# Making the low part of a weight tile one tile later than its high part, in a ten-stage fp32 network

## The chip, the cores and the metric

The kernel runs on one NeuronCore of a Trainium2 chip. The metric is the device time of one execution in microseconds (us). The engines are TensorE (PE, matrix products; PEld is its weight load), VectorE (DVE), ScalarE (ACT), GpSimd (POOL) and SyncE (SP, which here only issues DMAs). Each engine works through its own instruction stream strictly in order, so an instruction that waits for another engine also holds up everything behind it on its own.

## The reference, cut to what matters

256 tokens of width 1024 go through ten stages in float32: feed-forward, dilated attention, feed-forward, feed-forward, retention, feed-forward, and then twice a mixer and an MLP.

```python
def swiglu(h, w_gate, w_up, w_down):
    return (jax.nn.silu(h @ w_gate) * (h @ w_up)) @ w_down

# first block: two layers; the mixer is dilated attention, then retention
    h = swiglu(rms_norm(x, g[0]), ffn_w_gate[i, 0], ffn_w_up[i, 0], ffn_w_down[i, 0])   # 1024 -> 2816 -> 1024
    x = x + 0.5 * rms_norm(h, g[1])
    hm = rms_norm(x, g[2])
    m = dilated_attention(hm, ...) if i == 0 else retention(hm, ...)                    # hm @ w_in, heads, @ w_out
    x = x + rms_norm(m, g[3])
    h = swiglu(rms_norm(x, g[4]), ffn_w_gate[i, 1], ffn_w_up[i, 1], ffn_w_down[i, 1])
    x = x + 0.5 * rms_norm(h, g[5])

# second block: two layers
    dq, dk, dv, c_q, c_kv_kr, xq, gate_logits = jnp.split(h @ w_in[l], split_idx, axis=-1)
    y_diff = diff_attention(dq, dk, dv, ...) @ w_diff_o[l]       # q, k normed per head and rotated
    y_mla = latent_attention(c_q, c_kv_kr, ...) @ w_mla_o[l]
    y_mem = memory_cross_attention(xq, mem_n, w_mem_kv[l], ...) @ w_cross_o[l]
    merged = gates[:, :, 0] * y_diff + gates[:, :, 1] * y_mla + gates[:, :, 2] * y_mem
    x = x + merged @ w_out[l]
    x = x + jnp.square(jax.nn.relu(rmsnorm(x, g_mlp[l]) @ w_mlp1[l])) @ w_mlp2[l]
```

Every `@` with a weight matrix streams that matrix from memory once.

## The kernel before, in words

**Weights.** All weights are cut into 744 tiles, most of them 128 x 1024 float32 (512 KB), numbered in the order in which PE multiplies with them. A float32 product is made from three products of shorter numbers, so each tile is split in two. For tile i:

- SP loads it into `w_raw` (four buffers, `RAW`), once the low part of tile i-4 is made, which was the last to read that buffer;
- ACT copies it, rounded, into `w_hi` (L2205; four buffers, `SPLIT`), once PE has finished tile i-4;
- DVE makes `w_lo = w_raw - w_hi` (L2517), once `w_hi` is made. In the attention part of a mixer POOL does it for every second tile (L3240);
- PE does three matmuls for each 128-wide chunk: high x high, low x high, high x low (L1926, L1927, L1928; other places with the same pattern are L1952/L1953/L1961, L1909/L1910/L1915 and L1990/L1991/L1992). The first of the three waits for `w_lo` of the tile.

A 128 x 1024 tile keeps PE busy for some 2.8 us.

**The order.** The order of all work is planned once, as one list of steps (`self.plan`). Each engine's program goes through the whole list and issues the part of a step that is its own. So the list sets the order within each engine, and semaphores hold engines together. When PE's step of tile i has been planned, `tile_used(i)` plans `split(i + 4)`, one step that holds ACT's high part, DVE's or POOL's low part and SP's next load (tile i+8). At the end of a stage these steps can be held back (`hold_last`, `held`, `release`), so that they come after the work of the seam. Tiles which are multiplied in two halves of the tokens (`first_half`) are not followed by a split of their own.

**What lies between.** Attention steps are put into the same list between weight tiles by generators that take turns: on DVE these are evacuations of PSUM (L2559, L2575), norms (L3009, L3030, L3049), rotations of queries and keys (L3088 to L3096, six operations a half), maxima and scores (L2712), and in the dilated stage the weights of the three groups (L2822 to L2839). The exponentials stand on ACT (L2322, L2331, L2369), small powers on POOL (L3221).

**Tiles by stage.** 0 to 65 feed-forward, 66 to 145 dilated attention (on PE 217 to 511 us), 146 to 277 two feed-forwards, 278 to 357 retention (896 to 1161 us), 358 to 423 feed-forward, 424 to 519 first mixer (1350 to 1687 us), 520 to 583 MLP, 584 to 679 second mixer (1869 to 2206 us), 680 to 743 MLP. In the first mixer 436 is the second tile of the joint latent projection, 439 to 446 are queries, 447 to 454 keys, 455 to 462 values.

Of the kernel before, what the change touches and what calls it, by code (L numbers as in the profile page):

```python
# [399 lines left out]
class Kernel:  # L400


    def __init__(self, nc, a, stages):
# [49 lines left out]

        self.tiles, self.blocks, self.uid = [], 0, 0
        self.hold_at, self.held = None, []
        self.share, self.act_share, self.flip = 0, 2, 0
        self.gain_plan, self.gain_at = self.gains_in_order(), 0
        self.x_event = [[("x", 0, h, c) for c in range(2)] for h in range(HALVES)]
# [81 lines left out]
        return self.gain_at - 1  # L540

    def split(self, i):
        self.step("split", i, "pool" if self.share and i % self.share == 0 else "dve")

    def tile_used(self, i):
        if i == self.hold_at or self.held:
            self.held.append(i + SPLIT)
        else:
            self.split(i + SPLIT)
# [27 lines left out]
        return b  # L577

    def first_half(self, t, kind):
        self.tiles.append(t)  # L580
        self.tail.append((kind, len(self.tiles) - 1))
        self.step(kind, len(self.tiles) - 1, 0)
        yield
# [119 lines left out]
    def order(self):  # L703
        self.step("setup")
        self.step("load_x", 0)
        self.step("load", 0)
        self.step("load_x", 1)
        for i in range(1, RAW):
            self.step("load", i)
        self.step("next_gain", 1, [("x", 0, HALVES - 1, 1), ("w_raw", 1)])  # L710
        self.step("masks")
        for n, (kind, i, j) in enumerate(self.stages):
            self.st = n
            self.act_share = 3 if kind == "mix" else 2
            self.share = 0
            self.following = self.stages[n + 1] if n + 1 < len(self.stages) else None
            dict(ffn=self.ffn, mlp=self.mlp, dilated=self.dilated, retention=self.retention, mix=self.mix)[kind](i, j)
        for c in range(2):
            for half in range(HALVES):
                self.pending(half, c)  # L720
                self.step("store", half, c, self.x_event[half][c])
        self.plan = [s for s in self.plan if s[0] not in ("split", "load") or s[1] < len(self.tiles)]
        self.plan = [s for s in self.plan if s[0] != "next_gain" or s[1] < len(self.gain_plan)]


# [392 lines left out]
    def dilated(self, i, j):  # L1118
        a = self.a
        self.feed(order="classes")  # L1120
        self.step("masks_seen")
        q, k = self.put("da_q", 0, [P, HALVES, D]), self.put("da_k", 8, [P, HALVES, D])
        pairs = [(self.put(f"da_qt{n}", at, [P, DC, SEQ]), self.put(f"da_kt{n}", at + 8, [P, DC, SEQ])) for n, at in enumerate((16, 72))]
# [223 lines left out]
    def retention(self, i, j):  # L1347
# [17 lines left out]

        def qkv():
            bs = yield from self.pair_of_blocks(self.xt, (w_in, 0), (w_in, BLOCK))
            got["q"] = [[] for _ in range(HALVES)]
            for c, b in enumerate(bs):
                for half in range(HALVES):  # L1370
                    self.step("evac", Evac(b, half, self.by_turns(), q[:, half, c * BLOCK:(c + 1) * BLOCK], []))
                    got["q"][half].append(("evac", b.uid, half))
            got["k"] = yield from self.project(self.xt, w_in, D, D, k, D)
            got["v"] = yield from self.project(self.xt, w_in, D, H_R * DV_R, v, 2 * D)
# [176 lines left out]
    def mix(self, layer, _):  # L1551
# [20 lines left out]
        low = self.tok  # L1572
# [15 lines left out]
            mem_over.append(self.last_tile())  # L1588

        self.feed(memory_kv)  # L1590

        def projections():
            part = lambda name, dst, after=(): self.project(self.xt, w_in, D, IN_SIZES[name], dst, IN_AT[name], after)
# [242 lines left out]
def sp_program(k):  # L1836
    sp, q, ev = k.nc.sync, Queue(k.nc.sync), k.ev
    for what, *of in k.plan:
        if what == "load_x":
            c, = of  # L1840
            for half in range(HALVES):
                src = k.a["x"][0, half * P:(half + 1) * P, c * BLOCK:(c + 1) * BLOCK]
                sp.dma_start(k.x[:, half, c * BLOCK:(c + 1) * BLOCK], src).then_inc(*ev.mark(k.x_landed[half][c], ("x", 0, half, c), by=16))

        if what == "load":
            i, = of
            t = k.tiles[i]
            dst = k.raw[i % RAW][:, 0:t.nk * t.n].rearrange("p (k n) -> p k n", k=t.nk)
            if i >= RAW:
                q.wait_ge(*(yield from ev.of("w_lo", i - RAW)))  # L1850
            sp.dma_start(dst, t.view).then_inc(*ev.mark(k.w_landed[i % RAW], ("w_raw", i), by=16))
        if what == "split":
            i = of[0] + RAW
            if i < len(k.tiles):
                t = k.tiles[i]
                dst = k.raw[i % RAW][:, 0:t.nk * t.n].rearrange("p (k n) -> p k n", k=t.nk)
                q.wait_ge(*(yield from ev.of("w_lo", i - RAW)))
                sp.dma_start(dst, t.view).then_inc(*ev.mark(k.w_landed[i % RAW], ("w_raw", i), by=16))
        if what == "store":
            half, c, x_event = of  # L1860
            cols = slice(c * BLOCK, (c + 1) * BLOCK)
            q.wait_ge(*(yield from ev.of(*x_event)))
            q.wait_ge(*(yield from ev.of("masks")))
            sp.dma_start(k.out[0, half * P:(half + 1) * P, cols], k.x[:, half, cols]).then_inc(*ev.mark(k.out_stored, ("out", half, c), by=16))
        yield STEP
    q.wait_ge(*(yield from ev.of("out", HALVES - 1, 1)))
# [316 lines left out]
def act_program(k):  # L2183
# [8 lines left out]
    for what, *of in k.plan:  # L2192
# [3 lines left out]
                cols = slice(c * BLOCK, (c + 1) * BLOCK)  # L2196
                act.dma_start(k.gain_tile[0][:, cols], k.gain_plan[0][cols].partition_broadcast(P)).then_inc(*ev.mark(sem, (name, 0), by=16))

        if what == "split":
            i = of[0]  # L2200
            m = k.tiles[i].nk * k.tiles[i].n
            q.wait_ge(*(yield from ev.of("w_raw", i)))
            if i >= SPLIT:
                q.wait_ge(*(yield from ev.of("tile", i - SPLIT)))
            act.activation(k.w_hi[i % SPLIT][:, 0:m], k.raw[i % RAW][:, 0:m], ACT.Copy).then_inc(*ev.mark(k.w_hi_made, ("w_hi", i)))  # L2205
# [167 lines left out]
        if what == "oct_keep" and of[2] == "act":  # L2373
            o, s, _, dst = of
# [120 lines left out]
def dve_program(k):  # L2495
    dve, q, ev = k.nc.vector, Queue(k.nc.vector), k.ev
# [10 lines left out]
    for what, *of in k.plan:  # L2507
# [1 line left out]
            dve.memset(k.probs.free[0][0][:, :], 0.0).then_inc(*ev.mark(k.dve_done, ("fill_ready",)))  # L2509
            dve.memset(k.minus_half[:, :], -0.5).then_inc(*ev.mark(k.dve_done, ("minus_half",)))  # L2510

        if what == "split" and of[1] == "dve":
            i = of[0]
            m = k.tiles[i].nk * k.tiles[i].n
            q.wait_ge(*(yield from ev.of("w_hi", i)))
            hi, lo, raw = k.w_hi[i % SPLIT][:, 0:m], k.w_lo[i % SPLIT][:, 0:m], k.raw[i % RAW][:, 0:m]
            dve.tensor_tensor(lo, raw, hi.bitcast(F32), ALU.subtract).then_inc(*ev.mark(k.w_lo_made, ("w_lo", i)))  # L2517
# [278 lines left out]
        if what == "oct_keep" and of[2] == "dve":  # L2796
            o, s, _, dst = of
# [8 lines left out]
        if what in ("two_weights", "weights"):  # L2806
# [9 lines left out]
            low = k.da_low[:, at, :] if two else nm[:, 1, at, :]  # L2816
# [40 lines left out]
        if what == "combine":  # L2857
            o, s = of
# [356 lines left out]
def pool_program(k):  # L3215
# [7 lines left out]
    for what, *of in k.plan:  # L3223
# [8 lines left out]
            pool.dma_start(k.causal[:, :], a["c_causal"]).then_inc(*ev.mark(k.masks_landed, ("masks",), by=16))  # L3232
            q.wait_ge(*(yield from ev.of("minus_half")))

        if what == "split" and of[1] == "pool":
            i = of[0]
            m = k.tiles[i].nk * k.tiles[i].n
            q.wait_ge(*(yield from ev.of("w_hi", i)))
            hi, lo, raw = k.w_hi[i % SPLIT][:, 0:m], k.w_lo[i % SPLIT][:, 0:m], k.raw[i % RAW][:, 0:m]
            pool.tensor_tensor(lo, raw, hi.bitcast(F32), ALU.subtract).then_inc(*ev.mark(k.w_lo_pool, ("w_lo", i)))  # L3240
# [155 lines left out]
```

## Time and profile before

| | |
|---|---|
| time, median of 3 runs | 2388.45 us (2387.96 to 2388.94) |
| profiled execution: span | 2387.5 us |
| PE busy | 2351.7 us, 98% |
| PE's weight loads busy | 2020.1 us, 85% |
| DVE busy | 1511.0 us, 63% |
| ACT busy | 1195.5 us, 50% |
| POOL busy | 283.9 us, 12% |
| PE's granted clock | full (digit 9) in all 40 slices |
| memory read | 171 GB/s over the span |

The span runs from the first to the last recorded instruction of one execution; the timed runs lie 0.5 to 1.4 us above it. PE is busy nearly all the time, so a wait shows as a small gap on PE, and the sum of these gaps is what another order could win. DVE and ACT have idle time that costs nothing unless PE waits for what stands behind it.

### The profile page before, as it was taken

To read this page: it belongs to the slowest core of one execution; us is meant where nothing else is said; L and a number is where in the kernel's file an instruction comes from. 1 tells how busy PE (TensorE), PEld (TensorE's weight loads), DVE (VectorE), ACT (ScalarE), POOL (GpSimd) and SP (SyncE) were. 2 spreads that over 40 slices of the span, in tenths; PEclk is the share of its full clock that TensorE was granted. 3 is DMA by queue.
4 is the path that set the end of the run, shared out by engine and by line. 5 is a ranking of instruction groups with operands and counts; after the bars stand their busy time and mean duration, and the time that the engine had idled before them with its cause. 6 is when DMAs were issued, how large, how long until landed. Compare 5 with 4: busy or idle time off the path is not lost.

```text
span 2387.5 us, 34279 instructions
## 1 busy us (share of the span) xinstructions
PE 2351.7 (98%) x13900; PEld 2020.1 (85%) x13900; DVE 1511.0 (63%) x2307; ACT 1195.5 (50%) x1794; POOL 283.9 (12%) x247
## 2 busy tenths in 40 slices
PE   9999999999999999999999999999999999999999
PEld 8987778779979977777899887788998887888987
DVE  6555567776555658666665677756665687656654
ACT  4444454454444446444544565555554555554543
POOL 1100010000000000000001121434110122333000
PEclk9999999999999999999999999999999999999999
DMA  7755644466566656544666654445666554445554
GB/s 229 209 194 175 172 125 136 148 187 183 186 194 177 186 185 197 173 134 151 184 186 204 203 177 143 124 126 183 186 199 206 181 170 131 121 144 172 183 189 145
DMA packets 263278, 411.66 MB, mean 172 GB/s; under 512 B 13770, under 2 KB 129370, under 8 KB 263120
## 3 DMA queue, kind: packets, MB, share of 16 engines
q1 hardware_dynamic: 256256, 389.59, 53.2%
q0 software_dynamic: 6432, 19.28, 3.1%
q8 instruction: 110, 1.80, 0.3%
q10 hardware_dynamic: 432, 0.59, 0.1%
q14 instruction: 48, 0.39, 0.1%
HBM read 408.31 MB, written 1.10 MB: 171 GB/s over the span
## 4 chain that ended last, share of the span: by engine, by line
PE 85%; DVE 8%; ACT 4%; issue 1%; POOL 1%; DMA 0%; SPq 0%; ACTq 0%; DVEq 0%
PE banks L1926 16%; PE banks L1928 16%; PE banks L1927 16%; PE banks L1952 9%; PE banks L1961 9%; PE banks L1953 9%; DVE w_lo L2517 2%; ACT w_hi L2205 2%; PE banks L2015 1%; PE banks L2075 1%; PE banks L2028 1%; DVE probs L2712 1%; PE banks L1909 1%; PE banks L1910 1%; PE banks L1915 1%
## 5 line engine op out<-in xcount | busy, mean ns | idle before, releaser
L2517 DVE TENSOR_TENSOR w_lo<-w_raw,w_hi 128x1024 fp32r<-128x1024 f32 x688 | 838.9, 1225 | 618.1 <-ACT w_hi L2205 616.9
L2205 ACT ACTIVATE w_hi<-w_raw 128x1024 fp32r<-128x1024 f32 (+2 forms) x744 | 777.8, 1049 | 534.6 <-PE banks L1928 379.5
L1926 PE MATMUL banks<-w_hi,xt_hi 128*128 128x512 f32 (+2 forms) x1056 | 432.3, 409 | 7.0 <-DVE xt_lo L2545 3.6
L1952 PE MATMUL banks<-xt_hi,w_hi 128*128 128x256 f32 x1728 | 426.5, 283 | 4.7 <-DVE w_lo L2517 3.1
L1953 PE MATMUL banks<-xt_hi,w_lo 128*128 128x256 f32 x1728 | 425.2, 283 | 0.0
L1928 PE MATMUL banks<-w_hi,xt_lo 128*128 128x512 f32 (+2 forms) x1056 | 413.3, 391 | 0.0
L1927 PE MATMUL banks<-w_lo,xt_hi 128*128 128x512 f32 (+2 forms) x1056 | 412.4, 391 | 0.0
L1952 PEld LDWEIGHTS banks<-xt_hi,w_hi 128*128 128x128 f32 x1728 | 326.6, 189 | 6.6 <-DVE w_lo L2517 3.4
L1953 PEld LDWEIGHTS banks<-xt_hi,w_lo 128*128 128x128 f32 x1728 | 326.7, 189 | 0.0
L1926 PEld LDWEIGHTS banks<-w_hi,xt_hi 128*128 128x128 f32 x1056 | 198.9, 188 | 52.3 <-DVE w_lo L2517 9.0
L1961 PE MATMUL banks<-xt_lo,w_hi 128*128 128x256 f32 x1728 | 243.0, 282 | 0.0
L1928 PEld LDWEIGHTS banks<-w_hi,xt_lo 128*128 128x128 f32 x1056 | 198.9, 188 | 45.4
L1927 PEld LDWEIGHTS banks<-w_lo,xt_hi 128*128 128x128 f32 x1056 | 199.5, 189 | 41.8 <-issue 3.1
L1961 PEld LDWEIGHTS banks<-xt_lo,w_hi 128*128 128x128 f32 x1728 | 222.7, 189 | 0.0
L3221 POOL TENSOR_TENSOR stat<-stat,minus_half 128x1 f32<-128x1 f32 (+2 forms) x60 | 56.4, 944 | 1036.9 <-DVE stat L2505 549.2
L3240 POOL TENSOR_TENSOR w_lo<-w_raw,w_hi 128x1024 fp32r<-128x1024 f32 x56 | 134.5, 2402 | 263.8 <-ACT w_hi L2205 263.8
L1926 PE MATMUL banks<-w_hi,ffn_ht_hi 128*128 128x512 f32 x320 | 127.3, 398 | 0.0
L1928 PE MATMUL banks<-w_hi,ffn_ht_lo 128*128 128x512 f32 x320 | 126.5, 395 | 0.0
L1927 PE MATMUL banks<-w_lo,ffn_ht_hi 128*128 128x512 f32 x320 | 125.7, 393 | 0.0
L1928 PE MATMUL banks<-w_hi,mlp_ht_lo 128*128 128x512 f32 x256 | 101.7, 397 | 0.0
L1927 PE MATMUL banks<-w_lo,mlp_ht_hi 128*128 128x512 f32 x256 | 101.1, 395 | 0.0
L1926 PE MATMUL banks<-w_hi,mlp_ht_hi 128*128 128x512 f32 x256 | 100.9, 394 | 0.0
(438 smaller groups left out, 3042.4 us busy)
## 6 DMA issues: line engine op xcount, KB each, us to landing
w_raw<-in_w_mlp SPq DMA_DIRECT2D x128, 512.0 KB, 3.7
w_raw<-in_w_in SPq DMA_DIRECT2D x104, 512.0 KB, 3.7
w_raw<-in_ffn_w_gate SPq DMA_DIRECT2D x88, 512.0 KB, 3.9
w_raw<-in_ffn_w_up SPq DMA_DIRECT2D x88, 512.0 KB, 4.2
w_raw<-in_ffn_w_down SPq DMA_DIRECT2D x88, 512.0 KB, 3.6
w_raw<-in_attn_w_in SPq DMA_DIRECT2D x72, 512.0 KB, 3.8
w_raw<-in_ret_w_in SPq DMA_DIRECT2D x64, 512.0 KB, 3.8
w_raw<-in_ret_w_out SPq DMA_DIRECT2D x16, 512.0 KB, 3.8
```

What stands on the lines that cost most here:

```text
L1909: pe.matmul(bank, xh, hi[:, j * t.n:(j + 1) * t.n], start=(c == 0), stop=False)
L1910: pe.matmul(bank, xh, lo[:, j * t.n:(j + 1) * t.n], start=False, stop=False)
L1926: pe.matmul(bank, xh, wh, start=(c == 0), stop=False)
L1927: pe.matmul(bank, xh, wl, start=False, stop=False)
L1928: mm = pe.matmul(bank, xl, wh, start=False, stop=(c == b.chunks - 1))
L1952: pe.matmul(out[f], hi[:, cols], xh, start=(c == 0), stop=False)
L1953: pe.matmul(out[f], lo[:, cols], xh, start=False, stop=False)
L1961: mm = pe.matmul(out[f], hi[:, cols], xl, start=False, stop=(c == DC - 1))
L2205: act.activation(k.w_hi[i % SPLIT][:, 0:m], k.raw[i % RAW][:, 0:m], ACT.Copy).then_inc(*ev.mark(k.w_hi_made, ("w_hi", i)))
L2517: dve.tensor_tensor(lo, raw, hi.bitcast(F32), ALU.subtract).then_inc(*ev.mark(k.w_lo_made, ("w_lo", i)))
L3221: pool.tensor_tensor(out, mean, k.minus_half[:, 0:n], ALU.pow).then_inc(*ev.mark(k.pool_done, name))
L3240: pool.tensor_tensor(lo, raw, hi.bitcast(F32), ALU.subtract).then_inc(*ev.mark(k.w_lo_pool, ("w_lo", i)))
```

## The change

`split` is divided: the step "high" holds ACT's part, the step "low" DVE's or POOL's part and SP's load. With `low_later` set, the low part of a tile is put in the list only after the high part of the next tile; without it, straight behind its own, as before. It is set in the dilated stage from the end of `feed` on (the first tile concerned is 69), in retention from the end of the first pair of blocks on (tile 290), in the mixers from the end of the memory projection on (tiles 436 and 596). It is taken back at the start of every stage. Low parts that are due are put in the list at once where splits are held back and ahead of a tile in two halves.

```diff
@@ planner @@
     def split(self, i):
-        self.step("split", i, "pool" if self.share and i % self.share == 0 else "dve")
+        self.step("high", i)
+        self.low_parts()
+        self.low_due.append((i, "pool" if self.share and i % self.share == 0 else "dve"))
+        if not self.low_later:
+            self.low_parts()
+
+    def low_parts(self):
+        for i, by in self.low_due:
+            self.step("low", i, by)
+        self.low_due = []
 
     def tile_used(self, i):
         if i == self.hold_at or self.held:
+            self.low_parts()
             self.held.append(i + SPLIT)
         else:
             self.split(i + SPLIT)
@@ first_half @@
     def first_half(self, t, kind):
+        self.low_parts()
         self.tiles.append(t)
@@ order, for each stage @@
+            self.low_later = False
@@ dilated @@
         self.feed(order="classes")
+        self.low_later = True
@@ retention, qkv @@
             bs = yield from self.pair_of_blocks(self.xt, (w_in, 0), (w_in, BLOCK))
+            self.low_later = True
@@ mix @@
         self.feed(memory_kv)
+        self.low_later = True
@@ SP program @@
-        if what == "split":
+        if what == "low":
             i = of[0] + RAW
@@ ACT program @@
-        if what == "split":
+        if what == "high":
@@ DVE program; POOL program alike @@
-        if what == "split" and of[1] == "dve":
+        if what == "low" and of[1] == "dve":
```

The order of PE's, ACT's and SP's own instructions stays what it was. DVE's changes (180 low parts stand elsewhere), and POOL's in three places a mixer. In the rows below `w_lo0` to `w_lo3` are the four buffers: tile i is in buffer i mod 4.

DVE in the first mixer, at the joint latent projection: `w_lo0` is tile 436, `w_lo1` 437, `mx_ck` the normed keys of the memory; L2517 and L3049 become L2533 and L3065. Before:

```order
L2505 TENSOR_SCALAR stat17_97<-norm_sums1_105 128x4
L2517 TENSOR_TENSOR w_lo0_57<-w_raw0_49,w_hi0_53 128x864
L3049 TENSOR_TENSOR mx_ck0_216<-banks,stat16_96 128x512
L3049 TENSOR_TENSOR mx_ck0_216<-banks,stat18_98 128x512
L2517 TENSOR_TENSOR w_lo1_58<-w_raw1_50,w_hi1_54 128x864
L2517 TENSOR_TENSOR w_lo2_59<-w_raw2_51,w_hi2_55 128x576
```

and now:

```order
L2521 TENSOR_SCALAR stat17_97<-norm_sums1_105 128x4
L3065 TENSOR_TENSOR mx_ck0_216<-banks,stat16_96 128x512
L3065 TENSOR_TENSOR mx_ck0_216<-banks,stat18_98 128x512
L2533 TENSOR_TENSOR w_lo0_57<-w_raw0_49,w_hi0_53 128x864
L2533 TENSOR_TENSOR w_lo1_58<-w_raw1_50,w_hi1_54 128x864
L2575 TENSOR_SCALAR tok_64<-banks,row_scale_65 128x384
L2533 TENSOR_TENSOR w_lo2_59<-w_raw2_51,w_hi2_55 128x576
```

The low part of tile 436 stood ahead of the two `mx_ck` operations and now stands behind them; that of 438 has moved behind the evacuation of `tok`.

DVE in the same mixer, between the first and the second half of the key rotation (`mx_k`), where `w_lo3` is tile 459, `w_lo0` 460, `w_lo1` 461 and `w_lo2` 462. Before:

```order
L2517 TENSOR_TENSOR w_lo0_57<-w_raw0_49,w_hi0_53 128x1024
L3088 TENSOR_TENSOR tmp0_70<-mx_k0_207,rope_k_120 128x512
L3089 TENSOR_TENSOR tmp1_71<-mx_k0_207,rope_k_120 128x512
L3091 TENSOR_TENSOR mx_k0_207<-mx_k0_207,rope_k_120 128x16x32
L3092 TENSOR_TENSOR mx_k0_207<-mx_k0_207,rope_k_120 128x16x32
L3094 TENSOR_TENSOR mx_k0_207<-mx_k0_207,tmp0_70 128x16x32
L3096 TENSOR_TENSOR mx_k0_207<-mx_k0_207,tmp1_71 128x16x32
L2517 TENSOR_TENSOR w_lo1_58<-w_raw1_50,w_hi1_54 128x1024
L2517 TENSOR_TENSOR w_lo2_59<-w_raw2_51,w_hi2_55 128x1024
```

and now, where the row that stood at the head of these is tile 459's:

```order
L2533 TENSOR_TENSOR w_lo3_60<-w_raw3_52,w_hi3_56 128x1024
L3104 TENSOR_TENSOR tmp0_70<-mx_k0_207,rope_k_120 128x512
L3105 TENSOR_TENSOR tmp1_71<-mx_k0_207,rope_k_120 128x512
L3107 TENSOR_TENSOR mx_k0_207<-mx_k0_207,rope_k_120 128x16x32
L3108 TENSOR_TENSOR mx_k0_207<-mx_k0_207,rope_k_120 128x16x32
L3110 TENSOR_TENSOR mx_k0_207<-mx_k0_207,tmp0_70 128x16x32
L3112 TENSOR_TENSOR mx_k0_207<-mx_k0_207,tmp1_71 128x16x32
L2533 TENSOR_TENSOR w_lo0_57<-w_raw0_49,w_hi0_53 128x1024
L2533 TENSOR_TENSOR w_lo1_58<-w_raw1_50,w_hi1_54 128x1024
```

Tile 459's low part, made before the whole rotation until now, stands between its halves, and tile 460's behind both. At the query rotation, eight tiles earlier, the like happens to tile 452, which stood ahead of both halves and now stands behind them, and in retention to tile 297, which stood between the halves of the first query rotation.

DVE in the dilated stage, where the weights of the groups (`da_coef`) are made: `w_lo2` is tile 138, `w_lo3` 139, `w_lo0` 140. Before:

```order
L2836 RECIPROCAL da_part_155<-da_part_155 128x16
L2839 TENSOR_TENSOR da_coef_154<-da_coef_154,da_part_155 128x16 x2
L2517 TENSOR_TENSOR w_lo3_60<-w_raw3_52,w_hi3_56 128x1024
L2517 TENSOR_TENSOR w_lo0_57<-w_raw0_49,w_hi0_53 128x1024
L2559 TENSOR_SCALAR da_v0_148<-banks,row_scale_65 128x512
L2850 TENSOR_TENSOR tok_64<-tok_64,da_coef_154 128x512 x2
```

and now:

```order
L2852 RECIPROCAL da_part_155<-da_part_155 128x16
L2855 TENSOR_TENSOR da_coef_154<-da_coef_154,da_part_155 128x16 x2
L2533 TENSOR_TENSOR w_lo2_59<-w_raw2_51,w_hi2_55 128x1024
L2533 TENSOR_TENSOR w_lo3_60<-w_raw3_52,w_hi3_56 128x1024
L2575 TENSOR_SCALAR da_v0_148<-banks,row_scale_65 128x512
L2866 TENSOR_TENSOR tok_64<-tok_64,da_coef_154 128x512 x2
```

The low part of tile 138, which stood ahead of the group weights, now stands behind them and one place ahead of 139's; 140's has moved behind `da_v` and `tok`.

## Rows read from the trace of the kernel before

**Rows 1.** The page: span, and PE's granted clock in 40 slices.

```profile
span 2387.5 us, 34279 instructions
...
PEclk9999999999999999999999999999999999999999
```

**Rows 2.** The page, parts 5 and 6, on a tile's making.

```profile
L2517 DVE TENSOR_TENSOR w_lo<-w_raw,w_hi 128x1024 fp32r<-128x1024 f32 x688 | 838.9, 1225 | 618.1 <-ACT w_hi L2205 616.9
L2205 ACT ACTIVATE w_hi<-w_raw 128x1024 fp32r<-128x1024 f32 (+2 forms) x744 | 777.8, 1049 | 534.6 <-PE banks L1928 379.5
...
w_raw<-in_w_in SPq DMA_DIRECT2D x104, 512.0 KB, 3.7
```

**Rows 3.** PE's waits by releaser in the dilated stage: total us, times, longest.

```profile
PE banks L2136 <- DVE da_v L2559: 1.3, 1, 1.3
PE banks L2136 <- ACT probs_t L2369: 1.2, 1, 1.2
PE banks L2060 <- ACT probs L2322: 0.9, 1, 0.9
PE banks L2015 <- DVE tok L2873: 0.8, 1, 0.8
```

**Rows 4.** The same in retention.

```profile
PE banks L1990 <- DVE w_lo L2517: 1.4, 1, 1.4
```

**Rows 5.** The same in the first mixer.

```profile
PE banks L2060 <- ACT probs L2322: 3.5, 6, 1.4
PE banks L2028 <- DVE mx_nmax L2712: 1.1, 1, 1.1
```

**Rows 6.** DVE's waits in the dilated stage.

```profile
DVE w_lo L2517 <- ACT w_hi L2205: 77.8, 50, 3.1
```

**Rows 7.** DVE, timeline: start, duration, then [idle before <-releaser]; tile 436.

```profile
1379.81 0.69 DVE L3049 TENSOR_TENSOR mx_ck<-banks,stat 128x512 f32<-128x512 f32 x1 [0.38 <-POOL stat L3221]
1380.42 1.72 DVE L2517 TENSOR_TENSOR w_lo<-w_raw,w_hi 128x864 fp32r<-128x864 f32 x2
```

**Rows 8.** PE, timeline there.

```profile
1379.54 0.29 PE L1926 MATMUL banks<-w_hi,xt_hi 128*128 128x288 f32 x1
```

**Rows 9.** DVE at the query rotation, tiles 452 and 453.

```profile
1418.51 0.69 DVE L3088 TENSOR_TENSOR tmp<-mx_q,rope_q 128x512 f32<-128x512 f32 x1
...
1426.01 2.36 DVE L2517 TENSOR_TENSOR w_lo<-w_raw,w_hi 128x1024 fp32r<-128x1024 f32 x2
```

**Rows 10.** PE's first matmul of tile 452.

```profile
1424.44 0.40 PE L1926 MATMUL banks<-w_hi,xt_hi 128*128 128x512 f32 x1
```

**Rows 11.** DVE at the key rotation, tiles 460 and 461.

```profile
1446.66 1.22 DVE L2517 TENSOR_TENSOR w_lo<-w_raw,w_hi 128x1024 fp32r<-128x1024 f32 x1
...
1451.54 4.09 DVE L2517 TENSOR_TENSOR w_lo<-w_raw,w_hi 128x1024 fp32r<-128x1024 f32 x4
```

**Rows 12.** ACT ahead of it.

```profile
1436.38 1.26 ACT L2461 ACTIVATE tmp<-banks,row_scale 128x512 f32<-128x512 f32 x2
```

**Rows 13.** PE's first matmuls of tiles 460 and 461.

```profile
1448.79 0.39 PE L1926 MATMUL banks<-w_hi,xt_hi 128*128 128x512 f32 x1
...
1452.81 0.50 PE L1926 MATMUL banks<-w_hi,xt_hi 128*128 128x512 f32 x1 [1.05 <-DVE w_lo L2517]
```

**Rows 14.** Retention, DVE at tile 298.

```profile
946.78 3.49 DVE L2517 TENSOR_TENSOR w_lo<-w_raw,w_hi 128x1024 fp32r<-128x1024 f32 x3
```

**Rows 15.** Retention, PE's first matmul of tile 297.

```profile
944.90 0.40 PE L1926 MATMUL banks<-w_hi,xt_hi 128*128 128x512 f32 x1
```

**Rows 16.** Dilated stage: DVE at tile 139.

```profile
477.13 1.22 DVE L2517 TENSOR_TENSOR w_lo<-w_raw,w_hi 128x1024 fp32r<-128x1024 f32 x1
```

**Rows 17.** PE's first matmul of tile 138.

```profile
476.16 0.47 PE L1990 MATMUL banks<-w_hi,da_out_hi 128*128 128x512 f32 x1
```

**Rows 18.** Mixer attention: DVE's low part.

```profile
1514.73 2.00 DVE L2517 TENSOR_TENSOR w_lo<-w_raw,w_hi 128x1024 fp32r<-128x1024 f32 x1 [2.04 <-ACT w_hi L2205]
```

**Rows 19.** POOL's low part beside it.

```profile
1513.26 2.38 POOL L3240 TENSOR_TENSOR w_lo<-w_raw,w_hi 128x1024 fp32r<-128x1024 f32 x1
```

More of the change, by code:

```diff
@@ L455, in __init__ @@
         self.hold_at, self.held = None, []
+        self.low_due, self.low_later = [], False
         self.share, self.act_share, self.flip = 0, 2, 0
@@ L721, in order @@
                 self.step("store", half, c, self.x_event[half][c])
-        self.plan = [s for s in self.plan if s[0] not in ("split", "load") or s[1] < len(self.tiles)]
+        self.plan = [s for s in self.plan if s[0] not in ("high", "low", "load") or s[1] < len(self.tiles)]
         self.plan = [s for s in self.plan if s[0] != "next_gain" or s[1] < len(self.gain_plan)]
@@ L3233, in pool_program @@
             q.wait_ge(*(yield from ev.of("minus_half")))
-        if what == "split" and of[1] == "pool":
+        if what == "low" and of[1] == "pool":
             i = of[0]
```

## The prediction

> **What bounds the kernel now.** I read the page first. PE's clock is granted in full in every slice and the span is 2387.5 us [rows 1]; PE is busy nearly throughout, so the time is PE's own work plus its gaps, and a new order can only close gaps or open some. Then I read what a tile costs the other engines: DVE 1.225 us for the low part, ACT 1.049 us for the high part, 3.7 us for the load [rows 2]. The page also shows where DVE idles: 616.9 us of its 618.1 us ahead of a low part go to waiting for ACT's high part [rows 2]. In the dilated stage alone these are 77.8 us in 50 waits, the longest 3.1 us [rows 6]. That is no loss in itself. It matters where DVE work that PE needs stands behind such a wait. So the third view was PE's own waits, stage by stage [rows 3 to 5], and the fourth the timelines of DVE and PE around each low part that the new order puts behind longer work [rows 7 to 17]. For each I compared the end that the low part would have with PE's first matmul of that tile.
>
> **What the change does to each engine.** PE, ACT and SP issue what they did, in the same order; nothing is added or dropped. DVE meets each low part a step later, when its high part is long made, and so waits less there; that is the gain. But a low part can now land behind work that used to follow it; that is the loss, where the work is long.
>
> **The gain.** PE's short waits for attention chains come from DVE having stood at a low part while the scores or evacuations behind it were due.
> - Dilated stage: da_v 1.3, probs_t 1.2, probs 0.9, tok 0.8 [rows 3], together 4.2 us. Each of them is shorter than the longest stand of DVE (3.1 us). I take all, 4.2; the bounds are 2.1 (half of it, since a low part returns to the chain one place further on) and 4.2.
> - Retention: 1.4 us at L1990 [rows 4] is a wait for a low part that DVE made late behind a high part; I take 1.4, bounds 0 and 1.4.
> - A mixer: 3.5 + 1.1 = 4.6 us of waits for probs and maxima [rows 5]. Here the low part of the tile before lies in the same chain afterwards, ahead of the next maxima: nearly one low part in for each one out. I take 1.2 us a mixer, one stand of the seven, 2.4 for both; bounds 0 and 9.2.
>
> Together 8.0 us.
>
> **The loss.** Five places, two of the stages twice.
> - Mixer, tile 436. Its low part goes behind both mx_ck. The second of these waits for POOL and starts at 1379.81; DVE is free for the low part at 1380.42 [rows 7]. It is 864 wide, 864/1024 x 1.225 = 1.03 us, so it ends at 1381.5. PE takes the tile at 1379.54 [rows 8]. PE stops for 1.9 us. POOL's end is not moved by the change, so the bounds are 1.7 and 2.0.
> - Mixer, tile 452. The rotation of the queries, twelve operations, runs from 1418.51 to 1426.01 [rows 9], with no wait in it. The low part of 452 stood ahead of it and now stands behind: at the latest it ends at 1426.01 + 1.22 = 1427.2 where PE wants it at 1424.44 [rows 10], 2.8 us late. One low part fewer stands ahead of the rotation, which may start up to 1.2 us sooner if its inputs are there: 1.6 late. I take 1.9, since the norms' sums ahead of it still wait for ACT.
> - Mixer, tiles 459 to 461. The low part of 459 takes the slot at 1446.66 [rows 11]; PE wants 459 one tile of 2.8 us before 460, at 1448.79 - 2.81 = 1445.98 [rows 13]. It would end at 1447.88, 1.9 late. Again one low part has gone from ahead of the chain; its sums wait for ACT's squares, the last of them ready at 1436.38 + 1.26 = 1437.6 [rows 12], so that I count 0.7 of the 1.2 us: 1.2 late. Tile 460's low part then ends at 1451.54 + 1.22 - 0.7 = 1452.1, and PE, already 1.2 late, wants it at 1450.0: 2.1 more. In return the present stop of 1.05 us at 461 [rows 13], 1.2 with the slow start of the matmul, goes. Net 2.1; bounds 1.6 (all of the 1.2 us) and 2.8 (none).
> - Retention, tile 297. Its low part goes behind the second half of a rotation and takes the slot at 946.78 [rows 14]: the end is 948.0, less up to 0.9 for the low part gone from ahead; PE wants it at 944.90 [rows 15]. I take 2.2, bounds 2.2 and 3.1.
> - Dilated, tile 138. Its low part now follows the group weights, in the slot at 477.13 [rows 16], and ends at 478.35; PE wants it at 476.16 [rows 17]: 2.2 us, bounds 1.0 (if the weights come a low part sooner) and 2.2.
>
> A mixer loses 1.9 + 1.9 + 2.1 = 5.9 us, both 11.8; with 2.2 and 2.2 that is 16.2 us.
>
> **Loads.** SP's load of a tile is tied to a low part and so is issued about one tile, 2.8 us, later. Tile 452's low part was ready by 1418.6, where the rotation behind it begins [rows 9], and its use is at 1424.44 [rows 10]: 5.8 us of lead. The high part of the tile that is loaded then waits for PE to end 452, another 2.8 us, so a load had 8.6 us and keeps 5.8, against 3.7 us to land [rows 2]. Nothing, as long as the lead stays; where a low part is late by a rotation the load has less, and up to 1 us a place could be lost.
>
> **The sum.** 16.2 - 8.0 = +8.2 us on a span of 2387.5: 2395.7. The runs shown have a median of 2388.45, 0.95 above the span, so 2396.6, say 2396.5.
>
> **Ends.** All losses at their low end are (1.7 + 1.6 + 1.6) x 2 + 2.2 + 1.0 = 13.0, at their high end (2.0 + 2.8 + 2.8) x 2 + 3.1 + 2.2 = 20.5. Gains run from 2.1 to 14.8. So the ends are 2386.7 and 2406.9; of the likeliest case alone, with the mixer's gain near what I took, 2391 to 2402.
>
> **Rivals.**
> 1. *The attention chains win (faster).* Place: the seven waits a mixer of rows 5. If DVE, freed of its stands, runs ahead by a tile there, all of 9.2 us goes, with 4.2 and 1.4 elsewhere 14.8; and if it reaches the rotations sooner as well, half of the losses go, 8.1. Then 8.1 - 14.8 = -6.7: 2381.8. It decides from the point at which gains exceed losses by 4.8. For it speaks the size of the stands, 77.8 us in one stage [rows 6]; against it that no wait is seen inside the rotations, which are work, not waiting.
> 2. *They cancel.* Losses at their low end, 13.0, against gains of about 11: +2, 2390.5. For it speaks that the removed stand precedes most of the late low parts.
> 3. *DVE and POOL meet.* In a mixer's attention every second low part is POOL's. DVE's was made one tile time behind it; now DVE's of the tile before is due when POOL's begins. One such meeting is to be seen: POOL's from 1513.26 to 1515.64 [rows 19], DVE's from 1514.73 taking 2.00 us, not 1.22 [rows 18], that is 0.8 more. Were it so ahead of each of seven chains in both mixers, 11.2 more: 2407.7; ahead of half, 2402. Against it: only DVE's order is moved, and it is not held to the moment of the high part.
> 4. *The clock falls.* It is full in all slices [rows 1]. Should a stop of some 2 us bring it from 2.4 to 1.2 GHz for one tile, that tile costs 2.8 us more; over ten places 28: 2424. No row speaks for it.
>
> The Trainium skill, "SBUF — State Buffer", section "Who interferes with whom", says that a DVE instruction with two SBUF inputs contends with a GpSimd instruction that reads SBUF, and that whoever issues second is fully blocked. The pair of rows 18 and 19 agrees: 1515.64 + 1.22 = 1516.9, and DVE's ends at 1516.73. By that rule each meeting could cost up to POOL's whole 2.38 us, 33 us over fourteen; by the row it is 0.8 each.
>
> **Chances.** Forecast 0.47, chains win 0.18, cancel 0.25, DVE and POOL meet 0.08, clock 0.02. A measurement of this kernel tells 0.2%, 4.8 us, from no change. The forecast case is slower by more than that nine times in ten, rivals 3 and 4 always; cancelling is mostly within it, and a tenth beyond on either side. So slower 0.55, same 0.26, faster 0.19. The range leaves a tenth below and a tenth above: 2384.5 to 2404.
>
> **What would show it.** PE's waits should list new stops for low parts: at L1926 for tiles 436, 452, 459 and 460 in each mixer and 297 in retention, at L1990 for 138, each 1 to 2.5 us, some 16 us in all. Rows 3 and 4 should be gone or small, rows 5 nearly as they are. DVE's waits for the high part should shrink from 77.8 us in the dilated stage to under a quarter. I am wrong if the low parts at the rotations end in time, if the mixers' waits for probs fall by more than half, or if new waits stand at places other than these five.

## The result, and the profile after

The changed kernel takes 2396.96 us (median of 5 runs, 2396.47 to 2399.53) where the kernel before takes 2388.45: a ratio of 1.0038, 95% interval 1.0025 to 1.0051. It is slower by 8.5 us, clear of the 0.2% that can be told from no change. The forecast was 2396.5.

The page of the profiled execution, span and busy times:

```profile
span 2395.5 us, 34279 instructions
...
PE 2351.1 (98%) x13900; PEld 2019.6 (84%) x13900; DVE 1508.6 (63%) x2307; ACT 1196.5 (50%) x1794; POOL 290.6 (12%) x247
```

The number of instructions is that of before and PE's busy time is nearly so (2351.1 us, 2351.7 before); the 8.0 us of span are in PE's idle time, but for a stretch at a lower clock, which counts as busy and is told below. PE's waits in the dilated stage, by releaser (total us, times, longest; the lines are 16 higher than before the change):

```profile
PE banks L2006 <- DVE w_lo L2533: 2.1, 1, 2.1
PE banks L2105 <- POOL row_scale L3237: 1.2, 1, 1.2
```

The same in retention:

```profile
PE banks L1942 <- DVE w_lo L2533: 1.8, 1, 1.8
```

The same in the first mixer:

```profile
PE banks L1942 <- DVE w_lo L2533: 6.1, 4, 1.8
PE banks L2076 <- ACT probs L2338: 2.9, 4, 1.2
PE banks L2044 <- DVE mx_nmax L2728: 1.2, 1, 1.2
```

All four waits of [rows 3] and the one of [rows 4] are gone. In their place stand waits for low parts: one in the dilated stage, one in retention, four in the mixer. The mixer's waits for probs have only gone from 3.5 to 2.9 us [rows 5], but 1.2 of the 2.9 is a new wait (experiment 2); of the old ones 1.7 us are left. Those for the maxima are the same. One more wait had not been forecast: 1.2 us at L2105 for POOL's `row_scale`, where it was 0.3 us before.

DVE's own waits for the high part in the dilated stage:

```profile
DVE w_lo L2533 <- ACT w_hi L2221: 6.2, 5, 1.6
```

77.8 us [rows 6] have become 6.2. This is what the change was meant to remove, it did, and the time as a whole went up.

PE's first matmul of tile 138, 297, 436, 452, 459 and 460, in this order (timeline: start, duration, and in brackets the idle time before and what ended it):

```profile
474.82 0.48 PE L2006 MATMUL banks<-w_hi,da_out_hi 128*128 128x512 f32 x1 [2.10 <-DVE w_lo L2533]
...
944.35 0.50 PE L1942 MATMUL banks<-w_hi,xt_hi 128*128 128x512 f32 x1 [1.79 <-DVE w_lo L2533]
...
1378.79 0.40 PE L1942 MATMUL banks<-w_hi,xt_hi 128*128 128x288 f32 x1 [1.27 <-DVE w_lo L2533]
...
1425.79 0.50 PE L1942 MATMUL banks<-w_hi,xt_hi 128*128 128x512 f32 x1 [1.81 <-DVE w_lo L2533]
...
1448.78 0.47 PE L1942 MATMUL banks<-w_hi,xt_hi 128*128 128x512 f32 x1 [1.33 <-DVE w_lo L2533]
...
1453.56 0.50 PE L1942 MATMUL banks<-w_hi,xt_hi 128*128 128x512 f32 x1 [1.73 <-DVE w_lo L2533]
```

and the low part of tiles 452, 459 and 460 on DVE:

```profile
1424.51 2.35 DVE L2533 TENSOR_TENSOR w_lo<-w_raw,w_hi 128x1024 fp32r<-128x1024 f32 x2
...
1447.42 1.22 DVE L2533 TENSOR_TENSOR w_lo<-w_raw,w_hi 128x1024 fp32r<-128x1024 f32 x1
...
1452.29 2.35 DVE L2533 TENSOR_TENSOR w_lo<-w_raw,w_hi 128x1024 fp32r<-128x1024 f32 x2
```

The profile names the low part as what released each of these six matmuls, and for 452 it can be followed: 1424.51 + 1.22 = 1425.73, and PE goes on at 1425.79. Where PE had gone through 452 and 460 without a stop before [rows 10, 13], it now stands. To size the stops I laid PE's matmuls of the two executions side by side, one by one, which counts from start to start and so also takes in the slower first matmul behind a stop (the mixer's rows are those of the first mixer):

| place | forecast | measured |
|---|---|---|
| dilated, waits gone and other small gaps | -4.2 | -5.3 |
| dilated, L2105, `row_scale` | not seen | +0.9 |
| dilated, tile 138 | +2.2 | +2.4 |
| retention, L1990 gone | -1.4 | -1.7 |
| retention, tile 297 | +2.2 | +2.1 |
| mixer, tile 436 | +1.9 | +1.5 |
| mixer, tile 452 | +1.9 | +2.1 |
| mixer, tiles 459, 460, less the stop at 461 | +2.1 | +1.6 +2.0 -1.3 = +2.3 |
| mixer attention | -1.2 | -1.7 (-3.1, and +1.4 not seen) |
| second mixer, behind tile 612: PE's clock | rival 4, not in the sum | +1.5 |

By stage, from the drift of PE's matmuls at the stages' ends: dilated -2.0, retention +0.6, first mixer +4.2, second mixer +6.0, start of the kernel -0.7; together, before rounding, +8.0. The second mixer has the first one's terms (tile 596 +1.8, 612 +2.1, 619 and 620 +2.3, attention -1.7) and the clock's. The start is no effect of the change: up to tile 69 all versions in this document are the same program, and in their profiles the first 217 us come out between 1.1 us shorter and 1.1 us longer than in the kernel before. So about 1 us of each profiled span is chance.

### The profile page after: what moved, and what is told of

It is laid out like the page before. It is cut to its first block, busy times and chain, and to the rows that moved or that the text cites. A ratio compares the mean times of both kernels' runs of the same rounds, so it can differ in the third digit from the quotient of the medians.

```text
span 2395.5 us, 34279 instructions
## 1 busy us (share of the span) xinstructions
PE 2351.1 (98%) x13900; PEld 2019.6 (84%) x13900; DVE 1508.6 (63%) x2307; ACT 1196.5 (50%) x1794; POOL 290.6 (12%) x247
## 4 chain that ended last, share of the span: by engine, by line
PE 89%; DVE 8%; ACT 2%; POOL 1%; issue 1%; DMA 0%; SPq 0%; DVEq 0%; ACTq 0%
PE banks L1942 17%; PE banks L1944 16%; PE banks L1943 16%; PE banks L1968 9%; PE banks L1977 9%; PE banks L1969 9%; DVE w_lo L2533 2%; PE banks L2091 2%; PE banks L2031 1%; PE banks L2044 1%; PE banks L2076 1%; PE banks L2006 1%; PE banks L2007 1%; PE banks L2008 1%; PE banks L2188 1%; PE banks L1925 1%
## 5 line engine op out<-in xcount | busy, mean ns | idle before, releaser
L2533 DVE TENSOR_TENSOR w_lo<-w_raw,w_hi 128x1024 fp32r<-128x1024 f32 x688 | 844.0, 1235 | 422.0 <-ACT w_hi L2221 420.6
L3256 POOL TENSOR_TENSOR w_lo<-w_raw,w_hi 128x1024 fp32r<-128x1024 f32 x56 | 139.8, 2500 | 235.3 <-ACT w_hi L2221 235.3
```

## The experiments

All were timed in five rounds against the kernel before (experiments 4 and 8 with eleven runs of the version), but for three single executions at the end. The kernel before took 2388.7 us (median of 15 runs) beside the first four and 2388.82 beside the next four. Profiled spans are compared with 2387.5.

**1. The late low parts alone.** Everything as before the change, but the low parts of ten tiles go one step later.

```diff
-        if not self.low_later:
+        if not self.low_later or i not in (138, 297, 436, 452, 459, 460, 596, 612, 619, 620):
             self.low_parts()
```

> Only the low parts of ten tiles are made later than before (138; 297; 436, 452, 459, 460 and the same four of the second mixer, 596, 612, 619, 620); all other low parts stand where they stood. Theory (the loss is these places, each low part ending behind long work after PE wants it): no low part is taken from ahead of the rotations, so the high ends of my bounds hold: a mixer 1.9 + 2.8 + 1.9 + 2.1 less the 1.2 stop at 461 = 7.5, both 15.0; retention 3.1; dilated 2.2 less the da_v wait of 1.3 = 0.9; together +19.0, 2407.5 us, and up to 1.3 more for each stop behind which PE's clock falls. PE shows waits at exactly these tiles. Rival A (later slack takes the stops up again): under +8, below 2396.5. Rival B (the slowdown of the change comes from elsewhere in the mixers' attention, DVE against POOL): about 0, 2388.5.

Measured: 2404.3 us, ratio 1.0071 (1.0058 to 1.0083), span +15.1. PE's waits of the whole execution:

```profile
PE banks L1942 <- DVE w_lo L2533: 14.3, 9, 1.9
PE banks L2076 <- ACT probs L2338: 7.9, 13, 1.4
...
PE banks L2006 <- DVE w_lo L2533: 3.5, 2, 2.1
```

The chains' waits are those of before (L2076 is the old L2060: 8.0 us in 13 before, 7.9 in 13 now) and the stops are there alone. So ten instructions of 34,279, moved by one place in the list, cost 15 us; rivals A and B fall. The sum was 4 us too high (more than 5, if the clock's +1.5 below is left out), and for the most part for one reason: the late low part frees its own slot ahead of the long work, so that the work starts up to 1.2 us sooner. I had granted this in the prediction, for the low part of the tile before, and forgot it here. Tile 452 shows +1.6 where I wrote 2.8, tile 297 +2.1 where I wrote 3.1; 459 and 460, +2.0 each, were as written. These differences are 3.4 us in all; tile 436, +1.5 where I wrote 1.9, and a start of the kernel 1.0 us shorter make up most of the rest. On top comes +1.5 behind tile 297, where PE's clock fell, as the expectation allowed for:

```profile
947.00:948.00 1.00, 1.00 (x4) 0.80 0.23 39
948.00:951.00 3.00, 3.00 (x8) 0.50 0.94 311
951.00:952.00 1.00, 1.00 (x8) 1.00 1.01 361
```

(Columns: stretch, its length, PE's busy time and matmuls, granted clock, DMA share, GB/s.) 0.50 is the lower of the two levels, 1.2 GHz.

**2. The change without these ten.**

```diff
-        if not self.low_later:
+        if not self.low_later or i in (138, 297, 436, 452, 459, 460, 596, 612, 619, 620):
             self.low_parts()
```

> The whole change except that the low parts of those ten tiles stay straight behind their high parts. Theory (gain and loss are separate and add up): the changed kernel's gains without its stops: dilated -4.3, retention -1.5, each mixer -1.7: -9.2, 2379.2 us, and no fallen clock. Rival A (the attention waits vanished only because PE came late to them, held up by the stops): mixers 0, dilated -3, 2385. Rival B (the stops were not at these tiles): as the changed kernel, 2397.

Measured: 2380.32 us, ratio 0.9966 (0.9952 to 0.9979), span -9.5. The gains are there without the stops: -8.4 by the timed runs and -9.5 by the profile against -9.2 expected; rivals A and B fall. By stage the profile has -3.8 in the dilated stage (4.3 expected; 0.5 us of PE's wait at L2152 is left), -1.5 in retention and -1.7 in each mixer, together -8.7; the rest of the 9.5 is the kernel's start. The idea of the change is sound, and its cost hangs on ten places. With experiment 1: +15.6 and -8.4 add up to +7.2, the change measured +8.5 to +9.6. The two need not add up exactly, since both take away the same wait for `da_v` (1.4 us in the one, 0.8 in the other), which the change can take away only once.

Two kinds of spots are worse than before the change here too, though none of the ten late low parts is left: the wait for `row_scale` (experiment 6), and one in each mixer's attention. There PE loses 1.4 us, waiting for the exponentials behind DVE's maxima:

```profile
1496.23 0.52 PE L2076 MATMUL banks<-ident,probs 128*128 128x128 f32 x3 [1.20 <-ACT probs L2338]
```

DVE just ahead of it:

```profile
1487.93 0.69 DVE L3202 TENSOR_TENSOR tmp<-banks,stat 128x512 f32<-128x512 f32 x1
1488.66 2.42 DVE L3205 TENSOR_TENSOR mx_qt<-tmp 128x256 f32<-128x256 f32 x1
1491.00 3.39 DVE L2533 TENSOR_TENSOR w_lo<-w_raw,w_hi 128x1024 fp32r<-128x1024 f32 x1
1494.31 0.47 DVE L2728 CUSTOM_DVE_ANT_0 probs<-banks,causal,head_scale 128x256 f32<-128x256 f32 x1
```

and POOL at the same time:

```profile
1485.20 1.64 POOL L3237 TENSOR_TENSOR head_scale<-stat,minus_half 128x8 f32<-128x8 f32 x1 [5.76 <-DVE stat L2521]
1486.81 1.63 POOL L3237 TENSOR_TENSOR stat<-stat,minus_half 128x8 f32<-128x8 f32 x1
1488.41 4.90 POOL L3256 TENSOR_TENSOR w_lo<-w_raw,w_hi 128x1024 fp32r<-128x1024 f32 x2
```

The instruction that writes `mx_qt` subtracts one half of `tmp` from the other, so both its inputs lie in SBUF, as those of a low part do. It takes 2.42 us; in the kernel before:

```profile
1498.85 0.42 DVE L3189 TENSOR_TENSOR mx_qt<-tmp 128x256 f32<-128x256 f32 x1
```

The low part takes 3.39 us where [rows 2] have 1.225. Both lie beside POOL's two low parts, 4.90 us without a break from 1488.41 on. This is rival 3 of the prediction, in a form that I had not seen: not DVE's low part comes to POOL's, but two of POOL's come together. In the row of POOL, the order of before was low part, power, power, low part; the first of the two has moved behind the powers. DVE's subtraction ends just behind POOL's first low part, whose successor starts at 1490.75, and DVE's low part ends one length of its own behind the second. The rule of the Trainium skill ("SBUF — State Buffer", section "Who interferes with whom"), by which whichever of the two engines issues first takes what they share for its whole instruction and the other is fully blocked, agrees with both: half of the 4.90 us is 2.45, 1488.41 + 2.45 = 1490.86, and `mx_qt` ends at 1491.08; POOL's second ends at 1493.31, and 1.22 later, at 1494.5, DVE's low part is done (1494.39).

**3. The changed kernel once more.**

> The changed kernel once more, on the chip of the other three, with a second profile. Both theories: 2396.5 to 2399.5, +8 to +11. Its five runs stood in two groups 2.8 us apart at granted clocks of 0.998 and 0.997. If the difference is PE's clock falling behind one or two of the stops, a slow profile has one or two more stretches of some 3 us at 1.2 GHz behind stops at tiles 297, 436, 452, 459 or 460 than the first profile, which had one, behind tile 612; if it is memory, the stretches are the same and loads take longer.

Measured: 2398.33 us (2396.57 to 2399.98), ratio 1.0041 (1.0028 to 1.0053). The profiled execution, at 2396.86 us, was of the lower group, so it did not decide; experiment 9 bears on it.

**4. The dilated stage alone.** The two other `self.low_later = True` are left out.

> The change in the dilated stage alone. Theory (stages add up): -4.2 + 2.2 = -2.0, 2386.4 us, the stop at tile 138 as in the changed kernel. Rival (the dilated gain needs or feeds a later stage): another value between -5 and 0.

Measured: 2386.98 us, ratio 0.9993 (0.9984 to 1.0002), span -2.2. As expected in size, though the interval reaches no change.

**5. POOL's order restored.** As experiment 2, and POOL's low parts stay straight behind their high parts (edit against experiment 2).

```diff
-        self.low_due.append((i, "pool" if self.share and i % self.share == 0 else "dve"))
-        if not self.low_later or i in (138, ...):
+        by = "pool" if self.share and i % self.share == 0 else "dve"
+        self.low_due.append((i, by))
+        if not self.low_later or by == "pool" or i in (138, ...):
```

> As the kernel with ten tiles spared (2380.3 us), and besides every low part that POOL makes stands straight behind its high part again, so that POOL's order is that of the kernel before; only DVE's low parts are later. In the spared kernel POOL made two low parts back to back (1488.41, 4.90 us), a DVE operation of 0.42 us beside them took 2.42 and DVE's low part 3.39 instead of 1.22, and PE then lost 1.4 us, in both mixers. Theory (the moved POOL low parts make the two engines block each other): PE's +1.4 goes in each mixer, 2377.5 us, and no DVE low part takes over 2.1 us. Rival (DVE running earlier meets POOL whichever way POOL's order is): 2380.3, the long operations stay.

Measured: 2376.72 us, ratio 0.9949 (0.9937 to 0.9962), 3.6 us below experiment 2 where 2.8 were expected. The profiled spans differ by 1.8 us only, because the start of the kernel was 1.9 us longer here; the mixers are 1.8 and 1.9 us shorter. DVE and POOL at the place of the fences above:

```profile
1487.42 1.73 DVE L2522 TENSOR_SCALAR stat<-norm_sums 128x8 f32<-128x8 f32 x2
...
1491.40 0.43 DVE L3206 TENSOR_TENSOR mx_qt<-tmp 128x256 f32<-128x256 f32 x1
1491.74 1.22 DVE L2534 TENSOR_TENSOR w_lo<-w_raw,w_hi 128x1024 fp32r<-128x1024 f32 x1
```

```profile
1485.99 3.06 POOL L3257 TENSOR_TENSOR w_lo<-w_raw,w_hi 128x1024 fp32r<-128x1024 f32 x1 [6.05 <-ACT w_hi L2222]
1489.16 1.64 POOL L3238 TENSOR_TENSOR head_scale<-stat,minus_half 128x8 f32<-128x8 f32 x1
1490.77 1.63 POOL L3238 TENSOR_TENSOR stat<-stat,minus_half 128x8 f32<-128x8 f32 x1
1492.37 2.82 POOL L3257 TENSOR_TENSOR w_lo<-w_raw,w_hi 128x1024 fp32r<-128x1024 f32 x1
```

`mx_qt` is back at 0.43 us, the low part at 1.22. PE's +1.4 is gone in both mixers, and so is 1.0 us at a wait for the maxima; 0.5 us is lost against experiment 2 a little earlier, where `stat` stands beside POOL's first low part (1487.42, 1.73 us). That meeting is not new: it is the one of the kernel before, which came back with POOL's old order:

```profile
1492.91 2.18 DVE L2505 TENSOR_SCALAR stat<-norm_sums 128x8 f32<-128x8 f32 x2
```

So the rival falls as to the place, but meetings did not end. One low part of DVE in each mixer's attention still takes 3.39 us, where the expectation had none over 2.1, but no wait of PE stands behind it:

```profile
1511.25 3.39 DVE L2534 TENSOR_TENSOR w_lo<-w_raw,w_hi 128x1024 fp32r<-128x1024 f32 x1
```

**6. The start of the dilated stage spared too.** As experiment 5, with 69 and 70 among the tiles that stay straight.

> As the last kernel, and the low parts of tiles 69 and 70 also stay straight behind their high parts. At the start of the dilated stage the later low part of tile 70 ran beside POOL's small power operation, which took 1.46 us instead of 0.55, and PE waited 1.2 us for it instead of 0.3. Theory: another 0.9 us less, 2376.6 us. Rival (the stage's start is bound by ACT's sums, which have not moved): no difference to the last kernel, 2377.5.

The place in the changed kernel, POOL and then DVE:

```profile
221.33 1.46 POOL L3237 TENSOR_TENSOR row_scale<-stat,minus_half 128x1 f32<-128x1 f32 x1 [1.00 <-DVE stat L2521]
```

```profile
221.17 1.22 DVE L2533 TENSOR_TENSOR w_lo<-w_raw,w_hi 128x1024 fp32r<-128x1024 f32 x1
```

The low part of tile 70, which before the change was made ahead of the norms' sums (at 218.61), now starts 0.16 us before POOL's power for `row_scale`. That power takes 0.56 us for the other half of the tokens (at 219.77) and 1.46 us here; it ends only after DVE's 1.22 us. A DVE instruction of the size of a low part holds up a POOL instruction of one element a partition, and PE waits for that.

Measured: 2375.39 us, ratio 0.9943 (0.993 to 0.9955), span -13.4; PE's 0.9 us at this place are gone. Against experiment 5 it is 1.3 us in the medians, 0.9 was expected. The runs of the two versions overlap, so the timed difference proves little; the trace shows the 0.9 at the place. This is the fastest version: 13.4 us below the kernel before, 21.6 below the changed one.

**7. The mixers alone, 8. Retention alone.** Only the `self.low_later = True` of that stage is kept.

> The change in the two mixers alone. Theory (stages add up): the changed kernel's +8.0 of span less -2.0 (dilated) and +0.6 (retention) is +9.5, 2398 us, of which up to 1.3 for a fallen clock behind a stop and 2.8 for POOL against DVE. Rival (the mixers cancel, the loss is elsewhere): 2389.

> The change in retention alone. Theory: the stop of 2.1 us at tile 297 against the 1.4 us wait at L1990 that goes: +0.6, 2389.3 us. Rival (the stop is taken up by later waits): -1.5, 2387.2.

Measured: mixers 2399.75 us, ratio 1.0046 (1.0034 to 1.0059), span +10.7; retention 2390.14 us, 1.0005 (0.9996 to 1.0014), no difference by the runs, span +1.7. Both spans are above the expectation, by 1.2 and 1.1 us. In the mixers that is no other mechanism: first mixer +4.2, second +6.1, as in the changed kernel, and 0.6 us at the kernel's start, where the changed kernel, on whose total I had built the sum, was 0.7 faster. In retention PE's clock fell behind the stop at tile 297, which costs +1.5; the stop and the vanished wait are +2.1 and -1.7 as in the changed kernel.

**9. The changed kernel, three single executions**, each with a profile.

> The changed kernel again, one profile. Its runs stand in two groups, near 2396.7 (granted clock 0.998) and near 2399.7 (0.997). If a second fall of PE's clock makes the difference, an execution of the upper group shows two stretches at 1.2 GHz behind stops, each costing some 1.3 us, and one of the lower group shows one, behind tile 612. If not, the profile of an upper one shows the same single stretch and its extra time spread elsewhere.

> As the look before: one or two stretches at 1.2 GHz behind stops, the time going with their number.

> As the look before: one or two stretches at 1.2 GHz behind stops, and the time of the execution goes with their number.

Measured: 2399.44, 2398.09 and 2397.14 us. PE in windows, the first of them, behind the stop at tile 297:

```profile
943.00:944.00 1.00, 0.54 (x3) 1.00 0.49 186
946.00:947.00 1.00, 1.00 (x4) 0.55 0.70 100
947.00:949.00 2.00, 2.00 (x6) 0.50 0.95 316
949.00:950.00 1.00, 1.00 (x6) 0.74 1.03 350
```

and behind the one at tile 612:

```profile
1951.00:1952.00 1.00, 0.00 (x0) 1.00 0.00 0
1953.00:1956.00 3.00, 3.00 (x9) 0.50 0.81 238
1956.00:1957.00 1.00, 1.00 (x5) 0.78 0.77 285
```

The first, at 2399.44, has two falls to 1.2 GHz, behind 297 and 612. So has the second, at 2398.09. The third, at 2397.14, has one in its midst, behind 612, as the two profiles of 2396.79 and 2396.86 us had. The second fall is worth +1.5 us between the first execution here and the changed kernel's first profile; another 1.0 us between these two lies in the first 20 us of the kernel, where PE's granted clock is at the lower level for a while in every profile (between 16 and 18 us it is 0.58 here and 1.00 there). In the second the start is 0.4 us shorter than in the first profile, and with two falls it stands between the groups. So the one execution of the upper group that was profiled had a second fall of the clock and a slower start; what makes the start slower stays open.

## Why the prediction was right

- *PE's gaps are all there is to win or lose.* Nearly: PE's busy time is 2351.1 us against 2351.7. But busy time is not fixed: it was 2354.5 us in the execution with two falls of the clock, and 2347.8 in experiment 2.
- *The gain is in the waits of rows 3 and 4.* Shown: they are gone, and experiment 2 has their gain alone. The dilated stage gave about 1 us more than forecast: 0.6 of it at the four forecast places, which are worth 4.8 us from start to start and not 4.2, and the rest in small gaps, the largest 0.4 us ahead of another matmul on probs.
- *The mixer's attention gives little.* It gave -3.1 us and took 1.4 back, where DVE and POOL block each other; experiment 5 shows this by putting POOL's part back in its old place. The net of -1.7 is close to the 1.2 that I took, but for a reason I did not give for it: that is luck.
- *Five places lose.* Shown at each of them in the profile, and by experiment 1 as causes. The sizes are within 0.4 us everywhere. I ended each low part by the row of the operation that now stands in front. For a low part gone from ahead I took off only what that work's inputs allow: 0.7 of 1.2 us at the key rotation, since ACT's squares are ready at 1437.6 [rows 12]. With experiment 1 beside it, 0.5 of them came back there: tile 459 stops PE for 1.6 us in the changed kernel and for 2.0 in experiment 1.
- *At tile 436 the stop is 1.5, not 1.9 us* (1.8 at tile 596). The step that failed is "POOL's end is not moved by the change". POOL's second power, for which the second `mx_ck` waits, takes 1.01 us now and took 1.56 before:

```profile
1378.15 1.56 POOL L3221 TENSOR_TENSOR stat<-stat,minus_half 128x4 f32<-128x4 f32 x1
```

```profile
1375.97 1.01 POOL L3237 TENSOR_TENSOR stat<-stat,minus_half 128x4 f32<-128x4 f32 x1
```

Beside it stood, in the kernel before, the very low part that the change moves away:

```profile
1377.78 1.05 DVE L2517 TENSOR_TENSOR w_lo<-w_raw,w_hi 128x864 fp32r<-128x864 f32 x1
```

  In experiment 1, which moves this low part too, the power takes 1.01 us as well. So the change also ended a meeting of DVE and POOL, which the prediction had not looked for.
- *Rival 3, DVE and POOL meet.* It was given 0.08 as a whole and is true in one place of each mixer and at the start of the dilated stage, 3.7 us together: part of the sum, not another case. Its price for a meeting was too low: 0.8 us, where one made a DVE low part 2.2 us longer.
- *Rival 4, the clock falls.* 0.02 and "no row speaks for it" was too little. The digit 9 on the page is 90% or more of full speed, so "full in all slices" was read too strictly. The trace of the kernel before has a fall near its start, behind idle time of PE (columns as in experiment 1):

```profile
8.00:10.00 2.00, 0.17 (x2) 1.00 1.03 375
10.00:12.00 2.00, 0.69 (x3) 0.62 1.10 365
12.00:16.00 4.00, 4.00 (x21) 0.50 1.03 330
```

  In the changed kernel the clock fell behind one or two stops in every execution that was profiled. But it fell for some 3 us and cost about 1.5 us each time, not 2.8, and behind most stops it did not fall at all.
- *Loads cost nothing.* On PE none is seen: the places of the table, each with another releaser, make up the whole difference. ACT does wait longer for loads, for those of `in_w_in` 12.2 us instead of 4.3, in time that it had to spare. Moving the loads alone was not tested.
- *Its own signs.* By "I am wrong if new waits stand at places other than these five" it was wrong in three places: at `row_scale` and at one matmul on probs in each mixer.

The unforeseen terms are +0.9 (`row_scale`), +2.8 (the mixers' attention) and +1.5 (the clock), together +5.2; against them stand 1.1 us more gained in the dilated stage, 3.7 more in the mixers' attention before POOL took its part, a start 0.7 us faster, and smaller ones of 0.4 and less. So the mechanism was right in its places and signs, while the nearness of the total, 0.5 us, is luck: terms of 5 us on either side cancel, and one of them is the chance of the start.

## What to carry to other kernels

Moving a short instruction later in an in-order queue is paid not by the one place, but by the longest thing it lands behind: list every place where it crosses a run of work, and compare the end there with the consumer's first use, tile by tile. Apply such a rule everywhere but at those places; here ten exceptions turned +8.5 us into -8.4. When a queue is freed of waits, look at what it will then run beside: the three losses that were left in experiment 2, one in each mixer and one at the start of the dilated stage, all stood where DVE and POOL met, and the two edits against them gave another 5 us.

## What the hardware showed that was not expected

- DVE and POOL block each other for whole instructions, both ways: a DVE subtraction 0.42 us long took 2.42 and a low part of 1.22 took 3.39 beside two POOL low parts in a row, and a POOL power of 0.56 us took 1.46 beside a DVE low part, another 1.56 instead of 1.01.
- PE's granted clock fell from 2.4 to 1.2 GHz for some 3 us behind stops of about 2 us in start-to-start time (tiles 297 and 612), and not behind others as long (2.4 us at tile 138, 2.0 at 460); each fall cost about 1.5 us. It did so in all five profiles of the changed kernel behind tile 612, in two of them behind 297 too; with retention alone, and with the late low parts alone, behind 297, with the mixers alone behind 612. What decides between equal stops stays open.
